# Who makes the low parts of the weight tiles: VectorE alone instead of VectorE and GpSimd, and where they stand around the norms

## The chip, the cores and the metric

The kernel runs on one core of a Trainium2 chip. The time is the device time of one execution in microseconds (us). Engines: TensorE (PE, with PEld for its weight loads), VectorE (DVE), ScalarE (ACT), GpSimd (POOL), and SyncE (SP), whose queue issues most loads.

## What is computed

Four transformer layers over 256 tokens of width 1024, all in float32, batch 1. Layers 0 and 1 are of one model, layers 2 and 3 of another:

```python
# layers 0, 1
proj = x @ w_in[l]                       # 3352 columns, split in 12
mix  = concat([hgrn2(...), nsa(...)]) @ w_out[l]
x = layer_norm(ALPHA * x + mix, ln1_g[l], ln1_b[l])
ffn = (silu(x @ w_gate[l]) * (x @ w_up[l])) @ w_down[l]
x = layer_norm(ALPHA * x + ffn, ln2_g[l], ln2_b[l])
# layers 2, 3
h = rmsnorm(x, attn_norm[l]);  x = x + attention(h) @ w_o[l]
h = rmsnorm(x, ffn_norm[l]);   x = x + conv_ffn(h, ...)
# at the end: rmsnorm(x, final_norm)
```

Layer 2 mixes block attention with an attention over keys that an index score picks (the 64 best of each row); layer 3 adds three dilated patterns.

## The kernel before, in words

**Weights.** All big weights come as one stream of 206 tiles of 128 x 2048 float32 (1 MB each), in the order of use, into three raw buffers (`raw`, SLOTS = 3). A product in full float32 is made of three products in a shorter float: each operand is split into a high part (rounded) and a low part (the remainder), and `products` (lines 695 to 700) adds high by high, high by low and low by high. Each tile is split in two halves of 128 x 1024. ScalarE writes the high part (`split_high`, line 529, the copies at L537). The low part is `raw - w_hi`, two instructions per tile (`take_rest`, L551). It is made by VectorE for most tiles and by GpSimd for the 18 tiles in `on_pool` (lines 268 and 270). The split parts have three buffers too (PARTS = 3), so the split of tile i + 3 is issued right behind the use of tile i: `split_behind(eng, key, ...)` splits the tile that is three after `key`. The load of the tile that goes into a raw buffer waits for the low part of the tile in it (`load`, line 630, through `wait_split`).

**Tiles of GpSimd.** Around each of seven norms, the first and the third of the three tiles that follow the tail of the output product; and behind `nq1` in layers 0 and 1, `k0` and `v2` in layer 2, one tile each (POOL_AFTER).

**Around a norm.** The norms stand behind the output product ("out") and behind the down product ("down") of each layer. Tokens are in two row blocks, tt = 0 and tt = 1, of 128 tokens. TensorE adds up block 0, then block 1. VectorE norms block 0 (`norm(n, 0)`, L1433 to L1462: statistics, then two half rows), then TensorE turns the normed block (`x_transposes`, L762), ScalarE writes the high part of the turned block (`xT_out`, L569, a_hi) and VectorE the low part (L574, a_lo: the "turned remainders"). TensorE then multiplies block 0 with the first two of the new weight tiles (`behind_norm_tiles`, line 721, 24 products per tile), turns block 1 and multiplies it with the same two. So the second use starts no sooner than VectorE has normed block 1. The third new tile is used after that. The norm behind the down product of layer 1 is a double one: norms 3 and 4, a layer norm and an rms norm, one after the other.

The order of work on each engine is written out by hand; each engine runs its instructions in that order and waits on semaphores. Around a norm the order was:

- VectorE: norm of block 0; low part of the second tile; turned remainders of block 0; norm of block 1; turned remainders of block 1.
- ScalarE: root; high parts of the first and second tile; a_hi of block 0 (in the double norm the second root); high part of the third tile; root; a_hi of block 1.
- GpSimd: low part of the first tile; low part of the third tile.

**Layer 2, index attention.** While the projections run, VectorE also adds up index scores (`index_sums`, L1686 and L1688), picks the largest keys (`choose`, L1413 and L1414), takes logits (L1374, L1376) and copies turned probabilities for TensorE (L1387).

**GpSimd besides.** Differences of the decay levels (L1791), a gain (L1798), biases in layer 2 (L1819, L1820), the dilated bias for layer 3 (L1829), and the loads of the norms' gains.

Of the kernel before, what the change touches and what calls it, by code (L numbers as in the profile page):

```python
# [19 lines left out]
ALU = mybir.AluOpType  # L20
ACT = mybir.ActivationFunctionType
AX_X = mybir.AxisListType.X
F32 = mybir.dt.float32
# [10 lines left out]
LAYERS = 4  # L34
PIECES = 2 * NT
TILE = 2048
SLOTS = 3
PARTS = 3
# [197 lines left out]
def tail(l, kind):  # L236

    last = 3 if kind == "out" else FT // 2 - 1
    return [(l, f"{kind}{j}") for j in range(last - TAIL + 1, last + 1)]
# [9 lines left out]
    return key[1] in ("w1k", "w1v")  # L249


POOL_AFTER = {0: ["nq1"], 1: ["nq1"], 2: ["k0", "v2"]}


def turned(key):

    return key is not None and key[1:2] in (("xT",), ("oT",))
# [2 lines left out]
def build(nc, a):  # L260
# [4 lines left out]
    split_tiles = [key for key in stream if not unsplit(key)]  # L265
    split_no = {key: i for i, key in enumerate(split_tiles)}

    on_pool = {split_no[tail(l, kind)[i]] + PARTS for l in range(LAYERS) for kind in ("out", "down") for i in (0, 2)}

    on_pool |= {split_no[(l, n)] + PARTS for l in POOL_AFTER for n in POOL_AFTER[l]}  # L270
    turned_no = {key: i for i, key in enumerate(k for k, _ in bank_uses() if turned(k))}
    assert len(slots) == len(full_no) + 4 * LAYERS and len(tile_no) == len(stream)

    with ExitStack() as ctx:
# [3 lines left out]
        def sem(name):  # L278
            return ctx.enter_context(nc.semaphore(name))
# [118 lines left out]
        rows_used = sem("rows_used")  # L398
        w_hi_done = sem("w_hi_done")
        w_lo_done = sem("w_lo_done")  # L400
        w_lo_pool = sem("w_lo_pool")
        a_hi_done = sem("a_hi_done")
        a_lo_done = sem("a_lo_done")
        w_idx_loaded = sem("w_idx_loaded")
# [100 lines left out]
        def half_tile(i):  # L505
            return slice(i * (TILE // 2), (i + 1) * (TILE // 2))
# [32 lines left out]

        def wait_split(eng, i):  # L540

            mine = i in on_pool
            count = sum((j in on_pool) == mine for j in range(i + 1))
            eng.wait_ge(w_lo_pool if mine else w_lo_done, 2 * count)

        def take_rest(eng, i, done):

            t = tile_no[split_tiles[i]]
            for h in range(2):
                eng.wait_ge(w_hi_done, 2 * i + h + 1)  # L550
                eng.tensor_tensor(w_lo[:, i % PARTS, half_tile(h)], raw[:, t % SLOTS, half_tile(h)],  # L551
                                  w_hi[:, i % PARTS, half_tile(h)].bitcast(F32), ALU.subtract).then_inc(done, 1)

        def split_low(dve, i):
            if i not in on_pool:
                take_rest(dve, i, w_lo_done)

        def split_low_pool(pool, i):
            take_rest(pool, i, w_lo_pool)

        def split_behind(eng, key, split):

            i = split_no[key] + PARTS
            if i < len(split_tiles):
                split(eng, i)
# [511 lines left out]
        def _(act):  # L1077
# [25 lines left out]
            def xT_out(n, tt):  # L1103
                for q in range(2):
                    turned_high(act, (n, "xT", tt, q), a_hi[:, 4 * q:4 * q + 4, tt * P:(tt + 1) * P])

            def around_norm(l, kind, norms):

                keys, turn = tail(l, kind), norms[-1]
                act.activation(nstat[:, 0, 18:19], eps_ln[:, 0:1], ACT.Sqrt)  # L1110
                root(norms[0], 0)
                split_behind(act, keys[0], split_high)
                split_behind(act, keys[1], split_high)
                if len(norms) > 1:
                    root(turn, 0)
                elif turn != 8:
                    xT_out(turn, 0)
                split_behind(act, keys[2], split_high)
                if len(norms) > 1:
                    xT_out(turn, 0)  # L1120
                for n in norms:
                    root(n, 1)
                if turn != 8:
                    xT_out(turn, 1)
# [162 lines left out]
            for l in range(LAYERS):  # L1287
                for name in HEAD_TILES[l]:
                    (tile_out if l < 2 else qkv_out)(l, name)
                for step_ in plan(l):  # L1290
                    kind = step_[0]
# [37 lines left out]
        def _(dve):  # L1329
# [140 lines left out]
            def around_norm(l, kind, norms):  # L1470

                keys, turn = tail(l, kind), norms[-1]
                for n in norms:
                    norm(n, 0)
                split_behind(dve, keys[1], split_low)
                if turn != 8:
                    xT_out(turn, 0)
                for n in norms:
                    norm(n, 1)
                if turn != 8:  # L1480
                    xT_out(turn, 1)

            def feed_forward(l):
                for j in range(HEAD):
# [270 lines left out]
        @block.gpsimd  # L1755
        def _(pool):
            step = steps(pool, pool_step)
            pool.memset(s_hg, 0.0).then_inc(zeroed, 1)
            pool.memset(hid_v[:, :, :], 0.0).then_inc(zeroed, 1)
            pool.memset(cp[:, :, :, :], 0.0).then_inc(zeroed, 1)  # L1760
            pool.memset(ones[:, :], 1.0).then_inc(zeroed, 1)
            pool.memset(eps_ln[:, :], 1e-5)
            pool.memset(eps_rms[:, :], 1e-6).then_inc(zeroed, 1)

            def load_gains(g, b):
                pool.dma_start(gains[:, 0, :], g.partition_broadcast(P)).then_inc(gains_in, 16)
                if b is not None:
                    pool.dma_start(gains[:, 1, :], b.partition_broadcast(P)).then_inc(gains_in, 16)

            def next_gains(n, g, b=None):  # L1770
                pool.wait_ge(normed, n * PIECES)
                load_gains(g, b)

            def around_norm(l, kind):

                keys = tail(l, kind)
                split_behind(pool, keys[0], split_low_pool)
                split_behind(pool, keys[2], split_low_pool)

            load_gains(a["ln1_g"][0], a["ln1_b"][0])  # L1780
            for l in range(2):

                pool.wait_ge(cumsum_done, l + 1)
                for v in range(1, NLEV):
                    n = l * (NLEV - 1) + v
                    half = HALVES[v]
                    if v > 2:
                        pool.wait_ge(level_done, n - 2)
                    src = blocks(f_t, half)
                    mid = src[:, :, half - 1:half].to_broadcast([P, D // (2 * half), 2 * half])  # L1790
                    pool.tensor_tensor(blocks(dec[v % 2], half), src, mid, ALU.subtract).then_inc(diff_done, 1)  # L1791
                for name in POOL_AFTER[l]:
                    split_behind(pool, (l, name), split_low_pool)
                for i in range(2):
                    wait_drained(pool, (l, f"hg{i}"))
                for tt in range(NT):
                    g3 = g_hg[:, tt, :].rearrange("p (h v) -> p h v", h=HG_HEADS)
                    ins = pool.tensor_tensor(g3, g3, bc_mid(gnorm[:, l, :], HG_HEADS), ALU.mult)  # L1798
                ins.then_inc(g_scaled, 1)
                around_norm(l, "out")  # L1800
                next_gains(2 * l + 1, a["ln2_g"][l], a["ln2_b"][l])
                if l == 1:

                    pool.dma_start(gain4, a["rms_g"][0].partition_broadcast(P)).then_inc(gain4_in, 16)
                    pool.dma_start(w_idx_in, a["w_idx"]).then_inc(w_idx_loaded, 16)
                    pool.dma_start(score, a["causal"]).then_inc(score_in, 16)
                around_norm(l, "down")
                if l == 0:
                    next_gains(2, a["ln1_g"][1], a["ln1_b"][1])
            next_gains(5, a["rms_g"][1])  # L1810

            for name in POOL_AFTER[2]:
                split_behind(pool, (2, name), split_low_pool)
            pool.wait_ge(unsel_done, 1)
            for h in range(8):
                if h >= 2:
                    pool.wait_ge(logit_done, 2 * HEADS + 8 + h - 1)
                o = bias_s[h % 2]
                pool.tensor_tensor(o[:, 0:S], bias_of(16 + h, 1), unsel[:, 0:S], ALU.add)  # L1819
                pool.tensor_tensor(o[:, S:TRI], bias_of(16 + h, 0), unsel[:, S:TRI],  # L1820
                                   ALU.add).then_inc(bias_sel, 1)
            around_norm(2, "out")
            next_gains(6, a["rms_g"][2])

            pool.wait_ge(logit_done, 3 * HEADS)
            pool.dma_start(neglog, a["neglog"]).then_inc(neglog_in, 16)
            pool.wait_ge(neglog_in, 16)
            for h in range(16):
                ins = pool.tensor_tensor(bias_t[:, 8 + h, :], bias_t[:, 8 + h, :],  # L1829
                                         neglog, ALU.add)  # L1830
            ins.then_inc(bias_log, 1)
            around_norm(2, "down")
            next_gains(7, a["rms_g"][3])
            around_norm(3, "out")
            next_gains(8, a["final_g"])


# [135 lines left out]
```

## Time and profile before

| | us |
|---|---|
| median of 3 runs | 1594.84 (1592.29 to 1597.41) |
| profiled execution, its own time | 1594.35 |
| profiled execution, span | 1592.6 |
| TensorE busy | 1432.3 (90%) |
| VectorE busy | 975.0 (61%) |
| ScalarE busy | 696.5 (44%) |
| GpSimd busy | 173.2 (11%) |
| 16 DMA engines, queue of the weight stream | 39.2% |

All times of rows are from the start of the span in one profiled execution. An instruction's duration includes the time in which it is held up inside the engine; the time in brackets behind a row is the idle time of the engine before it and what ended it. The granted clock of TensorE (PEclk) has the levels 1.0 and 0.5 of full speed; a number between is a mean over the stretch.

### The profile page before, as it was taken

The numbers are of one execution on the slowest core, as the hardware profiler recorded it, in microseconds if no ns is written. First come the engines' busy times: TensorE is split into PE (matmuls) and PEld (weight loads), VectorE is DVE, ScalarE is ACT, GpSimd is POOL, SyncE is SP. The second block draws the span as 40 slices with busy tenths as digits, with TensorE's granted clock in tenths as the row PEclk, the third lists the DMA queues.
The fourth block names the chain that finished last, engine by engine and source line by source line (L and its number), as shares of the span: only waits on it lengthen the run. The fifth ranks groups of instructions, "written<-read, shape, count | busy, mean of one in ns | idle before, by whom it ended". The sixth has DMA issues, their size and how long they took to land.

```text
span 1592.6 us, 24395 instructions
## 1 busy us (share of the span) xinstructions
PE 1432.3 (90%) x9990; PEld 1334.0 (84%) x9990; DVE 975.0 (61%) x1625; ACT 696.5 (44%) x1136; POOL 173.2 (11%) x114
## 2 busy tenths in 40 slices
PE   6879779999996988899997989879999999799997
PEld 6878669999896977799996989679998898689996
DVE  4555555555757554665557467468767554567767
ACT  4453424333363452443342544245545454245543
POOL 0211020000203200300003013070000200200000
PEclk9879789999997988899997999999999999899999
DMA  8452115555451410455553433144554443235551
GB/s 299 143 213 80 37 70 186 185 185 186 159 184 55 159 54 27 133 212 186 186 185 119 159 107 131 56 149 172 184 200 167 169 149 112 83 138 194 186 208 54
DMA packets 37766, 233.21 MB, mean 146 GB/s; under 512 B 4920, under 2 KB 8712, under 8 KB 11032
## 3 DMA queue, kind: packets, MB, share of 16 engines
q1 hardware_dynamic: 35592, 224.18, 39.2%
q0 software_dynamic: 2064, 7.47, 1.4%
q8 instruction: 80, 1.31, 0.3%
q14 instruction: 30, 0.25, 0.0%
HBM read 230.55 MB, written 1.09 MB: 145 GB/s over the span
## 4 chain that ended last, share of the span: by engine, by line
PE 72%; DVE 17%; ACT 6%; issue 3%; DMA 2%; POOL 1%; DVEq 0%; ACTq 0%
PE bank L698 21%; PE bank L699 21%; PE bank L700 21%; DVE w_lo L551 5%; ACT w_hi L537 2%; PE bank L786 1%; DVE arena L1507 1%; DMA raw<-in_stream 1%; PE bank L798 1%; DVE x L1458 1%; DVE a_lo L574 1%; PE bank L860 1%; DVE res L1456 1%; POOL arena L1791 1%; PE bank L821 1%
## 5 line engine op out<-in xcount | busy, mean ns | idle before, releaser
L551 DVE TENSOR_TENSOR w_lo<-raw,w_hi 128x1024 fp32r<-128x1024 f32 x368 | 457.2, 1286 | 236.0 <-ACT w_hi L537 235.8
L698 PE MATMUL bank<-a_hi,w_hi 128*128 128x256 f32 x1856 | 530.9, 286 | 0.0
L699 PE MATMUL bank<-a_lo,w_hi 128*128 128x256 f32 x1856 | 526.7, 284 | 0.0
L700 PE MATMUL bank<-a_hi,w_lo 128*128 128x256 f32 x1856 | 526.3, 284 | 0.0
L537 ACT ACTIVATE w_hi<-raw 128x1024 fp32r<-128x1024 f32 x404 | 403.3, 1049 | 136.2 <-PE bank L700 79.1
L698 PEld LDWEIGHTS bank<-a_hi,w_hi 128*128 128x128 f32 x1856 | 357.8, 193 | 3.9 <-issue 0.9
L699 PEld LDWEIGHTS bank<-a_lo,w_hi 128*128 128x128 f32 x1856 | 357.7, 193 | 1.3
L700 PEld LDWEIGHTS bank<-a_hi,w_lo 128*128 128x128 f32 x1856 | 357.6, 193 | 0.0
L698 PE MATMUL bank<-w_hi,a_hi 128*128 128x256 f32 (+1 forms) x544 | 190.6, 350 | 51.3 <-DVE a_lo L574 38.8
L551 POOL TENSOR_TENSOR w_lo<-raw,w_hi 128x1024 fp32r<-128x1024 f32 x36 | 94.0, 2634 | 919.2 <-ACT w_hi L537 919.2
L699 PE MATMUL bank<-w_lo,a_hi 128*128 128x256 f32 (+1 forms) x544 | 183.5, 337 | 0.0
L700 PE MATMUL bank<-w_hi,a_lo 128*128 128x256 f32 (+1 forms) x544 | 182.7, 336 | 0.0
L698 PEld LDWEIGHTS bank<-w_hi,a_hi 128*128 128x128 f32 x544 | 117.8, 217 | 65.2 <-issue 47.2
L698 PE MATMUL bank<-w_hi,h_hi 128*128 128x512 f32 x352 | 139.8, 397 | 6.9 <-DVE h_lo L1520 4.1
L699 PE MATMUL bank<-w_lo,h_hi 128*128 128x512 f32 x352 | 140.9, 400 | 0.0
L700 PE MATMUL bank<-w_hi,h_lo 128*128 128x512 f32 x352 | 138.8, 394 | 0.0
L700 PEld LDWEIGHTS bank<-w_hi,a_lo 128*128 128x128 f32 x544 | 117.1, 215 | 7.0
L699 PEld LDWEIGHTS bank<-w_lo,a_hi 128*128 128x128 f32 x544 | 117.9, 217 | 5.9
L1507 DVE SCALAR_TENSOR_TENSOR arena<-bank,conv_col,arena 128x254 f32<-128x254 f32 (+1 forms) x176 | 76.7, 477 | 53.2 <-ACT arena L1148 51.5
L1082 ACT ACTIVATE arena<-bank 128x512 f32<-128x512 f32 (+2 forms) x56 | 32.9, 587 | 133.6 <-PE bank L700 133.5
L698 PEld LDWEIGHTS bank<-w_hi,h_hi 128*128 128x128 f32 x352 | 66.6, 189 | 23.3 <-DVE h_lo L1520 4.5
L700 PEld LDWEIGHTS bank<-w_hi,h_lo 128*128 128x128 f32 x352 | 66.4, 189 | 16.0
(230 smaller groups left out, 1487.4 us busy)
## 6 DMA issues: line engine op xcount, KB each, us to landing
raw<-in_stream SPq DMA_DIRECT2D x206, 1024.0 KB, 4.8
bias_t<-bias_rows SPq DMA_DIRECT2D x6, 512.0 KB, 7.5
gains<-in_ln_g POOLq DMA_DIRECT2D x4, 512.0 KB, 4.3
gains<-in_ln_b POOLq DMA_DIRECT2D x4, 512.0 KB, 6.3
gains<-in_rms_g POOLq DMA_DIRECT2D x3, 512.0 KB, 4.0
res<-in_xT SPq DMA_DIRECT2D x1, 1024.0 KB, 4.9
x<-in_x SPq DMA_DIRECT2D x1, 1024.0 KB, 8.3
out<-res SPq DMA_DIRECT2D x2, 512.0 KB, 2.6
```

What stands on the lines that cost most here:

```text
L537: act.activation(w_hi[:, i % PARTS, half_tile(h)], raw[:, t % SLOTS, half_tile(h)], ACT.Copy).then_inc(w_hi_done, 1)
L551: eng.tensor_tensor(w_lo[:, i % PARTS, half_tile(h)], raw[:, t % SLOTS, half_tile(h)], w_hi[:, i % PARTS, half_tile(h)].bitcast(F32), ALU. ...
L574: dve.tensor_tensor(part, bank_of(key).rearrange("p (i t) -> p i t", i=part.shape[1]), high.bitcast(F32), ALU.subtract).then_inc(*drained( ...
L698: pe.matmul(out, lh, rh, start=first, stop=False)
L699: pe.matmul(out, lh, rl, start=False, stop=False)
L700: return pe.matmul(out, ll, rh, start=False, stop=last)
L786: mm = pe.matmul(out[:, c:c + P], lhs[:, c:c + P], rhs[:, c:c + P], start=True, stop=True)
L798: mm = pe.matmul(b[:, 32 * i:32 * i + 30], w[:, k, :], blk[i][:, k, :, :].rearrange("p g n -> p (g n)"), start=(k == 0), stop=(k == CMP_KT ...
L821: mm = pe.matmul(b[:, c:c + NC], nq[lo:lo + DH, j, tt * P:(tt + 1) * P], kc2[lo:lo + DH, j // 2, :], start=True, stop=True)
L860: pe.matmul(b[i][:, 0:S], q[i][:, P:S], k[i], start=True, stop=True)
L1082: act.activation(dst, bank_of(key) if src is None else src, ACT.Copy, scale=scale).then_inc(*drained(key))
L1507: ins = dve.scalar_tensor_tensor(c[:, lag:], b[:, i * S:(i + 1) * S - lag], conv_col[:, m, i * FT + j, tap:tap + 1], c[:, lag:], ALU.mult, ...
```

## The change

GpSimd makes no low parts any more; VectorE makes those of all tiles, in the order of the stream, and one semaphore counts them. Behind `nq1`, `k0` and `v2` VectorE makes them at the place where it skipped them. Around a norm the order is new:

- VectorE: norm of block 0; low part of the first tile; turned remainders of block 0; low part of the second tile; norm of block 1; turned remainders of block 1; low part of the third tile.
- ScalarE: root; high part of the first tile; (second root in the double norm); a_hi of block 0; high parts of the second and third tile; root; a_hi of block 1.

```diff
-POOL_AFTER = {0: ["nq1"], 1: ["nq1"], 2: ["k0", "v2"]}
...
-    on_pool = {split_no[tail(l, kind)[i]] + PARTS for l in range(LAYERS) for kind in ("out", "down") for i in (0, 2)}
-    on_pool |= {split_no[(l, n)] + PARTS for l in POOL_AFTER for n in POOL_AFTER[l]}
...
         def wait_split(eng, i):
-            mine = i in on_pool
-            count = sum((j in on_pool) == mine for j in range(i + 1))
-            eng.wait_ge(w_lo_pool if mine else w_lo_done, 2 * count)
+            eng.wait_ge(w_lo_done, 2 * (i + 1))
...
+        def split_low(dve, i):
             t = tile_no[split_tiles[i]]
             for h in range(2):
-                eng.wait_ge(w_hi_done, 2 * i + h + 1)
-                eng.tensor_tensor(w_lo[:, i % PARTS, half_tile(h)], raw[:, t % SLOTS, half_tile(h)],
-                                  w_hi[:, i % PARTS, half_tile(h)].bitcast(F32), ALU.subtract).then_inc(done, 1)
+                dve.wait_ge(w_hi_done, 2 * i + h + 1)
+                dve.tensor_tensor(w_lo[:, i % PARTS, half_tile(h)], raw[:, t % SLOTS, half_tile(h)],
+                                  w_hi[:, i % PARTS, half_tile(h)].bitcast(F32), ALU.subtract).then_inc(w_lo_done, 1)
...
# ScalarE, around_norm
                 split_behind(act, keys[0], split_high)
-                split_behind(act, keys[1], split_high)
                 if len(norms) > 1:
                     root(turn, 0)
-                elif turn != 8:
+                if turn != 8:
                     xT_out(turn, 0)
+                split_behind(act, keys[1], split_high)
                 split_behind(act, keys[2], split_high)
-                if len(norms) > 1:
-                    xT_out(turn, 0)
...
# VectorE, around_norm
                 for n in norms:
                     norm(n, 0)
-                split_behind(dve, keys[1], split_low)
+                split_behind(dve, keys[0], split_low)
                 if turn != 8:
                     xT_out(turn, 0)
+                split_behind(dve, keys[1], split_low)
                 for n in norms:
                     norm(n, 1)
                 if turn != 8:
                     xT_out(turn, 1)
+                split_behind(dve, keys[2], split_low)
...
# GpSimd
-            def around_norm(l, kind):
-                keys = tail(l, kind)
-                split_behind(pool, keys[0], split_low_pool)
-                split_behind(pool, keys[2], split_low_pool)
...
-                for name in POOL_AFTER[l]:
-                    split_behind(pool, (l, name), split_low_pool)
...
-                around_norm(l, "out")
...
-                around_norm(l, "down")
```

## Rows read from the trace of the kernel before

**Rows 1.** Page: engines busy, chain of waits, GpSimd's subtractions, a load (KB, us).
```profile
PE 1432.3 (90%) x9990; PEld 1334.0 (84%) x9990; DVE 975.0 (61%) x1625; ACT 696.5 (44%) x1136; POOL 173.2 (11%) x114
...
PE 72%; DVE 17%; ACT 6%; issue 3%; DMA 2%; POOL 1%; DVEq 0%; ACTq 0%
...
L551 POOL TENSOR_TENSOR w_lo<-raw,w_hi 128x1024 fp32r<-128x1024 f32 x36 | 94.0, 2634 | 919.2 <-ACT w_hi L537 919.2
...
raw<-in_stream SPq DMA_DIRECT2D x206, 1024.0 KB, 4.8
```

**Rows 2.** Timeline (start, duration, instruction), VectorE, norm behind layer 0's output product.
```profile
225.88 2.96 DVE L1458 SCALAR_TENSOR_TENSOR x<-res,nstat,gains 128x512 f32<-128x512 f32 x1
228.77 2.84 DVE L1456 SCALAR_TENSOR_TENSOR res<-res,nstat,gains 128x512 f32<-128x512 f32 x1
...
232.31 2.35 DVE L551 TENSOR_TENSOR w_lo<-raw,w_hi 128x1024 fp32r<-128x1024 f32 x2
234.58 1.28 DVE L574 TENSOR_TENSOR a_lo<-bank,a_hi 128x512 fp32r<-128x512 f32 x2
235.78 0.67 DVE L1433 SCALAR_TENSOR_TENSOR res<-x,bank 128x512 f32<-128x512 f32 x1
...
241.68 0.75 DVE L1458 SCALAR_TENSOR_TENSOR x<-res,nstat,gains 128x512 f32<-128x512 f32 x1
```

**Rows 3.** Timeline, GpSimd and TensorE, same norm.
```profile
225.89 5.17 POOL L551 TENSOR_TENSOR w_lo<-raw,w_hi 128x1024 fp32r<-128x1024 f32 x2 [60.36 <-ACT w_hi L537]
...
235.41 0.55 PE L698 MATMUL bank<-w_hi,a_hi 128*128 128x256 f32 x1 [2.13 <-DVE a_lo L574]
...
245.26 0.36 PE L698 MATMUL bank<-w_hi,a_hi 128*128 128x256 f32 x1 [1.07 <-DVE a_lo L574]
```

**Rows 4.** Timeline, norm behind layer 0's down product, VectorE and TensorE.
```profile
427.51 4.55 DVE L551 TENSOR_TENSOR w_lo<-raw,w_hi 128x1024 fp32r<-128x1024 f32 x2
...
439.20 0.75 DVE L1458 SCALAR_TENSOR_TENSOR x<-res,nstat,gains 128x512 f32<-128x512 f32 x1
...
440.78 0.36 PE L698 MATMUL bank<-w_hi,a_hi 128*128 128x256 f32 x1
```

**Rows 5.** Timeline, double norm behind layer 1's down product.
```profile
844.74 2.78 DVE L1458 SCALAR_TENSOR_TENSOR x<-res,nstat,gains 128x512 f32<-128x512 f32 x1
...
851.65 6.65 DVE L551 TENSOR_TENSOR w_lo<-raw,w_hi 128x1024 fp32r<-128x1024 f32 x2
...
871.22 0.55 PE L698 MATMUL bank<-w_hi,a_hi 128*128 128x256 f32 x1 [0.84 <-DVE a_lo L574]
```

**Rows 6.** Timeline, norm behind layer 2's output product.
```profile
1038.21 5.40 DVE L551 TENSOR_TENSOR w_lo<-raw,w_hi 128x1024 fp32r<-128x1024 f32 x2 [1.23 <-ACT w_hi L537]
...
1048.76 1.42 DVE L1462 SCALAR_TENSOR_TENSOR res<-x,nstat,gains 128x512 f32<-128x512 f32 x2
...
1054.20 0.36 PE L698 MATMUL bank<-w_hi,a_hi 128*128 128x256 f32 x1 [1.07 <-DVE a_lo L574]
```

**Rows 7.** Windows: us; busy of PE, PEld, DVE, ACT, POOL; clock; DMA; GB/s.
```profile
245.20:251.20 6.00, 5.94 (x50) 5.97 (x50) 1.74 (x3) 2.49 (x3) 0.00 (x0) 1.00 0.35 115
859.00:867.40 8.40, 8.34 (x48) 8.16 (x48) 7.77 (x14) 0.30 (x1) 0.00 (x0) 0.68 0.66 252
```

**Rows 8.** Timeline, layer 0, VectorE behind nq1.
```profile
129.89 1.31 DVE L1353 COPY_PREDICATED arena<-hg_mask,bank 128x1024 f32<-128x1024 uint8 x1 [4.57 <-PE bank L786]
```

**Rows 9.** Timeline, layer 2: VectorE and TensorE behind k0, TensorE behind v2.
```profile
922.50 1.42 DVE L1686 SCALAR_TENSOR_TENSOR arena<-arena,gates 128x256 f32<-128x256 f32 x1 [3.58 <-ACT arena L1277]
923.83 2.46 DVE L1688 SCALAR_TENSOR_TENSOR arena<-arena,gates 128x128 f32<-128x128 f32 x1
926.39 0.48 DVE L1686 SCALAR_TENSOR_TENSOR arena<-arena,gates 128x256 f32<-128x256 f32 x1
...
930.59 0.70 PE L893 MATMUL bank<-arena 64*128 64x256 f32 x4 [2.39 <-ACT arena L1277]
...
964.05 0.41 PE L882 MATMUL bank<-arena,pT 128*128 128x64 f32 x2 [1.13 <-DVE pT L1387]
```

More of the change, by code:

```diff
@@ L400, in build @@
         w_lo_done = sem("w_lo_done")
-        w_lo_pool = sem("w_lo_pool")
         a_hi_done = sem("a_hi_done")
@@ L540, in wait_split @@
         def wait_split(eng, i):
-            mine = i in on_pool
-            count = sum((j in on_pool) == mine for j in range(i + 1))
-            eng.wait_ge(w_lo_pool if mine else w_lo_done, 2 * count)
-        def take_rest(eng, i, done):
+            eng.wait_ge(w_lo_done, 2 * (i + 1))
+        def split_low(dve, i):
             t = tile_no[split_tiles[i]]
             for h in range(2):
-                eng.wait_ge(w_hi_done, 2 * i + h + 1)
-                eng.tensor_tensor(w_lo[:, i % PARTS, half_tile(h)], raw[:, t % SLOTS, half_tile(h)],
-                                  w_hi[:, i % PARTS, half_tile(h)].bitcast(F32), ALU.subtract).then_inc(done, 1)
[L554 to L559, printed above, removed]
+                dve.wait_ge(w_hi_done, 2 * i + h + 1)
+                dve.tensor_tensor(w_lo[:, i % PARTS, half_tile(h)], raw[:, t % SLOTS, half_tile(h)],
+                                  w_hi[:, i % PARTS, half_tile(h)].bitcast(F32), ALU.subtract).then_inc(w_lo_done, 1)
         def split_behind(eng, key, split):
@@ L1810, in _ @@
             next_gains(5, a["rms_g"][1])
-            for name in POOL_AFTER[2]:
-                split_behind(pool, (2, name), split_low_pool)
             pool.wait_ge(unsel_done, 1)
@@ L1821, in _ @@
                                    ALU.add).then_inc(bias_sel, 1)
-            around_norm(2, "out")
             next_gains(6, a["rms_g"][2])
@@ L1831, in _ @@
             ins.then_inc(bias_log, 1)
-            around_norm(2, "down")
             next_gains(7, a["rms_g"][3])
-            around_norm(3, "out")
             next_gains(8, a["final_g"])
```

## The prediction, as it was put on record before the run

> **What bounds the kernel now.** I read the page first: TensorE is busy 90% of the span, and the chain of waits that ended last is TensorE for 72% and VectorE for 17%, with GpSimd at 1% [rows 1]. So the kernel is a stream of products with places where TensorE stands and VectorE is the one it stands for. GpSimd's 36 subtractions (18 tiles, two halves each) take 94.0 us on GpSimd, 2.63 us each [rows 1]. Taken by engine shares they look free. I then asked for the waits of TensorE by stretch, and for the timeline of all engines around each of the seven norms at which GpSimd subtracts, and at the other four tiles.
>
> The timeline shows that they aren't free. In the first norm VectorE's scaling of a half row takes 0.75 us when GpSimd is quiet (at 241.68) but 2.96 and 2.84 us at 225.88 and 228.77; these start just as GpSimd's pair of subtractions does and end with its two halves [rows 2, 3]. That is 2.2 + 2.1 = 4.3 us of VectorE standing still inside instructions, on the path norm, turned block, a_lo, first product. The same shows at the tile's own subtractions: two halves take 2.35 us on VectorE alone [rows 2], 4.55 [rows 4], 6.65 [rows 5] and 5.40 us [rows 6] with GpSimd on its own pair. Instructions that read PSUM for one input aren't held: L1433 took 0.67 us at 235.78 and a_lo 1.28 for two, while GpSimd made its second tile [rows 2].
>
> **What of it counts.** The products of block 1 (tt = 1) start when VectorE has normed block 1. In the norm behind layer 0's down product the last scaling ends at 439.20 + 0.75 = 439.95 and the first product of block 1 starts at 440.78 [rows 4]: 0.83 us later. I call this the norm-bound start. Where TensorE came to block 1 later than that, it was still at the products of block 0, and there is slack: in layer 0's first norm 245.26 - (241.68 + 0.75 + 0.83) = 2.0 us [rows 2, 3], and in layer 2's first 1054.20 - (1048.76 + 1.42 + 0.83) = 3.2 us [rows 6].
>
> **The seven norms.** In the new order VectorE does, ahead of the norm of block 1, one pair of halves more (2.35 us), and loses the stalls.
> - Layer 0, out: stalls 4.3, less 2.35: norm of block 1 starts about 1.9 us sooner. The products of block 0 start at about 231.1 in place of 235.41 (norm of block 0 done at 225.88 + 3 x 0.75 = 228.1, first tile's low part at 230.4, the first a_lo 0.65 later) and no longer cover block 1, so the 2.0 of slack come too: 3.9 us. The high part of the second tile, now behind a_hi on ScalarE, is wanted 24 products after 231.1, at 234 or later, and VectorE has its low part by 234.1. Layer 1, out, is of the same form: 3.9.
> - Layer 0, down: 2.0 in one L1458 (as the 2.78 - 0.75 of [rows 5]) and 2.2 in the subtractions (4.55 - 2.35 [rows 4]), less 2.35: 1.9, and no slack; with a small hold in the second norm 2.0 us.
> - Layer 1, down (double norm): 2.03 in L1458 and 4.3 in the subtractions [rows 5], less 2.35: 4.0, and some 0.4 in a small instruction between; 4.4 us off the start at 871.22.
> - Layer 2, out: 5.40 - 2.35 = 3.05 in the subtractions, and VectorE's idle 1.23 us before them [rows 6] is now used; less 2.35 and less some 0.7 for waits on a_hi and on the second tile's high part, which ScalarE makes later: 1.2. Plus the slack 3.2 (0.2 kept back for the first half row): 4.2 us. Layer 3, out, has the same form: 4.2.
> - Layer 2, down: between the down norm of layer 0 and the out norm of layer 2, as TensorE has the last rows to add between the turns and the products: 3.1.
> Sum: 3.9 + 3.9 + 2.0 + 4.4 + 4.2 + 4.2 + 3.1 = 25.7 us.
>
> **TensorE's clock.** 48 products took 5.94 us at clock 1.00, and 8.34 us at a mean of 0.68, behind a stand of 5.89 us [rows 7]: 2.4 us more. After 1.07 us of idle they ran at 1.00 (the start at 245.26 [rows 3, 7]). Before, the slow ones were mostly those of block 0. In the new order block 0 starts sooner and is done sooner, and then TensorE waits 2 to 4 us for the norm of block 1, so in some norms the slow level (1.2 GHz) will fall on the products of block 1, which count. Bounds: 0 and 7 x 2.4 = 17 us. I take 4 us, nearer to 0, because the wait is broken by the turns of the first half, and because where block 0 itself runs slow it fills the wait.
>
> **The third tile.** Its low part moves behind the turned remainders of block 1. TensorE wants it 48 products (5.94 us [rows 7]) after that start, and VectorE has it 1.28 + 2.35 us after the norm, some 3 us early: nothing. Its raw buffer comes free about 5 us later than from GpSimd, so SyncE issues the load of the tile three further that much later, with everything behind it in its queue; a load lands 4.8 us after issue [rows 1], and the tile's high part is written only behind the use of the third tile, more than 10 us on: nothing.
>
> **The other four tiles.** Behind nq1 in layers 0 and 1 VectorE stood idle 4.57 us for TensorE [rows 8], and the pair fits there: 0. Behind k0 in layer 2 GpSimd held an index sum for 1.42 + 2.46 us where the next pair starts with 0.48 and goes on at a like rate, about 3.1 us of stall; VectorE's own pair costs about 1.1 net of its idle time before: 2.0 us gained, of the 2.39 that TensorE stood [rows 9]. Behind v2 VectorE works without a gap at choosing keys, with nothing in it that GpSimd held, so 2.35 us go straight into the wait for pT (1.13 before [rows 9]), which becomes 3.5; with such a stand the clock may fall, 1.3 more. Net of layer 2: +1.7 us; bounds -2.0 (the pair at v2 absorbed) and +4 (k0 brings nothing, v2 all).
>
> **A page on this.** The Trainium skill, SBUF — State Buffer, section Who interferes with whom, has GpSimd and a VectorE instruction with two SBUF inputs share one read interface, held for the whole instruction, so that the other blocks fully. Taken by that, each of the some 16 held instructions would lose a whole GpSimd half (5.17 / 2 = 2.6 us), not 2.1 to 2.2, and with some 6 us more in the sum the time would be 1568, on the side of the second rival. The rows measure the stall itself, so I keep to them.
>
> **Sum.** -25.7 + 4.0 + 1.7 = -20.0 us. The profiled execution took 1594.35 us (0.49 less than the median of the runs shown): 1574.4 us. All of the gain lies on the path in places where TensorE stood, and what follows (feed-forward products at clock 1.00) is shifted as a whole.
>
> **Rivals.**
> - The clock eats most of it: the slow level falls on block 1 in nearly all norms (some 12 us) and layer 2 costs 4: -25.7 + 12 + 3 = -11: 1584. For it: TensorE's wait before block 1 gets longer in all seven. Against it: the start at 440.78 followed a norm-bound wait and was at full clock. Chance 0.15.
> - More than that: no clock loss, and layer 2 even: 1594.4 - 27.7 = 1567. Chance 0.17.
> - The stalls aren't GpSimd's doing, but come with the loads that land then; GpSimd's leaving changes nothing for them, while the new order still swaps places: within 0.3%. Against it: the holds start and end with GpSimd's halves. Chance 0.03.
> - Slower: the third tile. If its raw buffer, free some 5 us later, is what the stream waits for, then every norm loses 5 us at the tile three further and the gain at the norm is given back and more: 7 x 5 = 35 us against 20 gained: 1609. It decides when the load lands later than ScalarE's turn at it; of the 10 us above 4.8 go to the load, so some 5 us of room are left, and the DMA engines' share is at 0.35 to 0.66 [rows 7]. Chance 0.05.
> - The forecast: 0.60.
>
> About 0.3% (5 us) is what a measurement of this kernel can tell from no change. Range: from 1564 (the third case with its bounds) to 1584. Faster 0.92, within 0.3% 0.03, slower 0.05.
>
> **What would show it.** GpSimd has no L551 and some 80 us busy. VectorE's L551 has 404 instructions at a mean of about 1.2 us. L1456, L1458 take 0.75 us in all norms. The first product of block 0 follows the norm some 4 us sooner in each out norm, and 7 in the double one; the first product of block 1 starts about 0.8 us behind the last scaling in all seven. The wait of L882 for pT in layer 2 grows to 3 us or more. Wrong would be: a scaling longer than 1 us with no GpSimd near it, a wait of L698 for the third tile, or a slow clock in block 1 everywhere.

## The result: 1574.07 us, and the profile after

The changed kernel takes 1574.07 us (median of 4 runs, 1571.35 to 1574.62), the kernel before in the same comparison 1594.41 us: a ratio of 0.9867, 95% interval 0.9848 to 0.9887. It is 20.3 us faster; 1574.4 was forecast. The profiled execution has a span of 1572.8 us.

The page of the changed kernel, which answers to [rows 1]: busy times, the chain of waits, VectorE's low parts, a load.
```profile
PE 1428.0 (91%) x9990; PEld 1329.7 (85%) x9990; DVE 985.0 (63%) x1661; ACT 696.8 (44%) x1136; POOL 77.6 (5%) x78
...
PE 72%; DVE 17%; ACT 5%; issue 3%; DMA 2%; POOL 1%; DVEq 0%; SPq 0%; ACTq 0%
...
L542 DVE TENSOR_TENSOR w_lo<-raw,w_hi 128x1024 fp32r<-128x1024 f32 x404 | 484.3, 1243 | 225.7 <-ACT w_hi L530 225.0
...
raw<-in_stream SPq DMA_DIRECT2D x206, 1024.0 KB, 4.9
```
GpSimd's subtractions are gone. VectorE got 36 of them, some 42 us of work by the 2.35 us that a pair takes, and is busy only 10 us longer: for the other 32 us it had stood still inside its own instructions. The chain has nearly the shares of before, so it does not tell where 20 us went; the timelines do.

VectorE in the norm behind layer 0's output product, changed kernel (start, duration, instruction), which answers to [rows 2]:
```profile
222.91 0.75 DVE L1438 SCALAR_TENSOR_TENSOR res<-res,nstat,gains 128x512 f32<-128x512 f32 x1
223.70 0.76 DVE L1440 SCALAR_TENSOR_TENSOR x<-res,nstat,gains 128x512 f32<-128x512 f32 x1
...
225.82 2.35 DVE L542 TENSOR_TENSOR w_lo<-raw,w_hi 128x1024 fp32r<-128x1024 f32 x2
228.09 1.28 DVE L558 TENSOR_TENSOR a_lo<-bank,a_hi 128x512 fp32r<-128x512 f32 x2
229.28 2.35 DVE L542 TENSOR_TENSOR w_lo<-raw,w_hi 128x1024 fp32r<-128x1024 f32 x2
231.55 0.68 DVE L1415 SCALAR_TENSOR_TENSOR res<-x,bank 128x512 f32<-128x512 f32 x1
...
237.32 0.75 DVE L1440 SCALAR_TENSOR_TENSOR x<-res,nstat,gains 128x512 f32<-128x512 f32 x1
...
240.58 2.35 DVE L542 TENSOR_TENSOR w_lo<-raw,w_hi 128x1024 fp32r<-128x1024 f32 x2
```
TensorE there, and in the norms behind layer 0's down product, layer 1's down product (double) and layer 2's output product, one after the other; these answer to [rows 3 to 6]. In brackets is the idle time before a row:
```profile
228.92 0.36 PE L682 MATMUL bank<-w_hi,a_hi 128*128 128x256 f32 x1 [1.92 <-DVE a_lo L558]
...
236.77 0.63 PE L746 MATMUL bank<-ident,x 128*128 128x128 f32 x4 [1.86 <-DVE x L1440]
...
238.96 0.56 PE L682 MATMUL bank<-w_hi,a_hi 128*128 128x256 f32 x1
...
432.51 0.63 PE L746 MATMUL bank<-ident,x 128*128 128x128 f32 x4 [1.08 <-DVE x L1440]
...
434.64 0.36 PE L682 MATMUL bank<-w_hi,a_hi 128*128 128x256 f32 x1
...
846.70 0.36 PE L682 MATMUL bank<-w_hi,a_hi 128*128 128x256 f32 x1 [2.24 <-DVE a_lo L558]
...
859.00 1.94 PE L746 MATMUL bank<-ident,res 128*128 128x128 f32 x8 [6.33 <-DVE res L1444]
861.60 0.55 PE L682 MATMUL bank<-w_hi,a_hi 128*128 128x256 f32 x1 [0.65 <-DVE a_lo L558]
...
1041.64 1.29 PE L746 MATMUL bank<-ident,res 128*128 128x128 f32 x8 [1.39 <-DVE res L1444]
1043.77 0.36 PE L682 MATMUL bank<-w_hi,a_hi 128*128 128x256 f32 x1 [0.84 <-DVE a_lo L558]
```
The 2.96 and 2.84 us of [rows 2] are 0.75 us now, and each pair of subtractions takes 2.35. TensorE is done with block 0 before VectorE has normed block 1, so it stands ahead of the turns (L746): 1.9, 1.1, 6.3 and 1.4 us.

I took the n-th product of TensorE in both traces and the difference of their starts (after less before). Its steps over the places of the prediction, in us:

| place | predicted | measured |
|---|---|---|
| layer 0: out, down | -3.9, -2.0 | -2.6, -2.2 |
| layer 1: out, down | -3.9, -4.4 | -1.8, -3.9 |
| layer 2: out, down | -4.2, -3.1 | -3.9, -3.9 |
| layer 3: out | -4.2 | -4.6 |
| clock behind the norms | +4 | (within the rows above) |
| layer 2 at k0; at v2 | -2.0; +3.7 | -2.1; +3.9 |
| elsewhere | 0 | +1.4 |
| sum | -20.0 | -19.7 |

"Elsewhere" is -1.3 up to layer 0's norm, +2.4 inside layer 1, +1.0 in layer 2 beside the two tiles and -0.75 in its feed-forward part. TensorE ran the same instructions there, and slow stretches of its clock fell at other moments. In layer 1 one wait for VectorE grew as well, from 1.31 to 2.92 us: TensorE came to it sooner, out of faster products, and VectorE's work ahead of it was bound by ScalarE.

TensorE's clock in block 1's products, changed kernel (us; busy of PE, PEld, DVE, ACT, POOL; clock; DMA share; GB/s), in the norms of layer 0 out and down, layer 1 out and down, and layer 2 out (the third row starts with the turns of the second half row):
```profile
238.90:244.90 6.00, 6.00 (x32) 6.00 (x32) 2.96 (x3) 1.05 (x2) 0.59 (x2) 0.55 0.62 199
434.64:440.64 6.00, 6.00 (x50) 6.00 (x51) 4.23 (x5) 3.07 (x4) 0.52 (x1) 1.00 0.71 220
657.52:663.52 6.00, 6.00 (x39) 6.00 (x40) 3.49 (x4) 1.64 (x3) 2.70 (x5) 0.74 0.75 184
861.60:869.31 7.71, 7.71 (x50) 7.71 (x51) 4.22 (x5) 2.49 (x3) 0.00 (x0) 0.75 0.55 192
1043.77:1049.77 6.00, 6.00 (x50) 6.00 (x51) 4.07 (x4) 2.49 (x3) 3.06 (x4) 1.00 0.63 214
```
50 products in 6.00 us at 2.4 GHz, 32 in the same time where most of it was at 1.2. Before, layer 0's block 1 ran at 1.00 [rows 7]: this is why that norm gave 2.6 us of 3.9. (At the start of block 1 it was 5.0 us ahead, 0.8 of them from a slow stretch that no longer fell just ahead of the norm; the slow products took 2.4 back.) In the double norm block 1 ran at the lower level for a while in the kernel before, too:
```profile
871.20:878.60 7.40, 7.38 (x49) 7.40 (x50) 1.70 (x3) 2.49 (x3) 0.00 (x0) 0.77 0.20 68
```
So against the kernel before, block 1's 48 products take longer by 2.4 us in layer 0's out norm, 1.1 in layer 1's and 0.2 in the double one: 3.7 us, and nothing in the other four.

Layer 2 behind v2, where VectorE's new pair has no cover; TensorE's row and the clock behind it, answering to the last of [rows 9]:
```profile
954.33 0.66 PE L866 MATMUL bank<-arena,pT 128*128 128x64 f32 x2 [3.42 <-DVE pT L1369]
```
```profile
954.30:959.30 5.00, 4.97 (x23) 5.00 (x24) 4.73 (x15) 2.46 (x5) 0.00 (x0) 0.50 0.01 2
```

### The profile page after: what moved, and what is told of

Read it like the earlier page. It is cut to its first block, busy times and chain, and to the rows that moved or that the text cites. A ratio compares the mean times of both kernels' runs of the same rounds, so it can differ in the third digit from the quotient of the medians.

```text
span 1572.8 us, 24395 instructions
## 1 busy us (share of the span) xinstructions
PE 1428.0 (91%) x9990; PEld 1329.7 (85%) x9990; DVE 985.0 (63%) x1661; ACT 696.8 (44%) x1136; POOL 77.6 (5%) x78
## 3 DMA queue, kind: packets, MB, share of 16 engines
q8 instruction: 80, 1.31, 0.3%
## 4 chain that ended last, share of the span: by engine, by line
PE 72%; DVE 17%; ACT 5%; issue 3%; DMA 2%; POOL 1%; DVEq 0%; SPq 0%; ACTq 0%
PE bank L682 21%; PE bank L683 21%; PE bank L684 21%; DVE w_lo L542 5%; DMA raw<-in_stream 2%; ACT w_hi L530 2%; PE bank L770 2%; DVE arena L1491 1%; PE bank L782 1%; PE bank L844 1%; DVE a_lo L558 1%; DVE nstat L1420 1%; DVE x L1440 1%; PE bank L868 1%; PE bank L867 1%
## 5 line engine op out<-in xcount | busy, mean ns | idle before, releaser
L542 DVE TENSOR_TENSOR w_lo<-raw,w_hi 128x1024 fp32r<-128x1024 f32 x404 | 484.3, 1243 | 225.7 <-ACT w_hi L530 225.0
L682 PE MATMUL bank<-w_hi,a_hi 128*128 128x256 f32 (+1 forms) x544 | 186.3, 343 | 32.1 <-DVE a_lo L558 19.7
L683 PE MATMUL bank<-w_lo,a_hi 128*128 128x256 f32 (+1 forms) x544 | 179.6, 330 | 0.0
L684 PE MATMUL bank<-w_hi,a_lo 128*128 128x256 f32 (+1 forms) x544 | 178.3, 328 | 0.0
L682 PEld LDWEIGHTS bank<-w_hi,a_hi 128*128 128x128 f32 x544 | 113.3, 208 | 45.1 <-issue 27.2
L684 PEld LDWEIGHTS bank<-w_hi,a_lo 128*128 128x128 f32 x544 | 112.9, 208 | 7.1
L683 PEld LDWEIGHTS bank<-w_lo,a_hi 128*128 128x128 f32 x544 | 113.3, 208 | 5.7
L1212 ACT ACTIVATE lbuf<-lbuf,mxn 128x256 f32<-128x256 f32 x64 | 32.6, 509 | 106.5 <-DVEq L1360 106.0
```

Of the source, the lines that this page charges most:

```text
L542: dve.tensor_tensor(w_lo[:, i % PARTS, half_tile(h)], raw[:, t % SLOTS, half_tile(h)], w_hi[:, i % PARTS, half_tile(h)].bitcast(F32), ALU. ...
L682: pe.matmul(out, lh, rh, start=first, stop=False)
L683: pe.matmul(out, lh, rl, start=False, stop=False)
L684: return pe.matmul(out, ll, rh, start=False, stop=last)
L1212: act.activation(e[:, 0:S], e[:, 0:S], ACT.Exp, scale=-1.0, bias=mxn[:, half, 1, h:h + 1], accum_out=esum[:, half, 1, h:h + 1])
```

## The experiments

Twelve kernels ran, in three comparisons, in which the kernel before took 1594.05, 1592.63 and 1594.45 us; differences of 1 or 2 us between kernels of different comparisons mean nothing. The theory: GpSimd's subtractions hold those VectorE instructions that read two inputs in SBUF, and taking them away frees VectorE's path to the norm of block 1. The rivals: the order is what gains; the stalls aren't GpSimd's; the clock takes the gain.

**The move and the order, each alone.** "engine_alone" is the changed kernel with the old order:
```diff
 split_behind(dve, keys[0], split_low)
+split_behind(dve, keys[1], split_low)
 if turn != 8:
     xT_out(turn, 0)
-split_behind(dve, keys[1], split_low)
```
(and ScalarE's order of before). 

> All low parts on VectorE, but around the norms the order of before: both low parts of the first two tiles stand ahead of the turned remainders of block 0 (and ScalarE has the old order too). If the gain is GpSimd's holds going away, nearly all of it stays: VectorE reaches the norm of block 1 at the same time as in the changed kernel, block 0's products start 2.35 us later, and that only shows where TensorE waited less than 2.35 us ahead of block 1 (1.86, 1.86, 1.08, 6.33, 1.39, 1.40 and 0 us in the seven norms): at most 0.5+0.5+1.3+0+1.0+1.0+2.35 = 6.6 us, of which TensorE's clock gives some back as it stands for less: 1578 us, range 1574 to 1581. If the new order is what gains, this kernel stays near the one before: 1590 us or more.

Measured: 1578.76 us, ratio 0.9899 (0.9886 to 0.9912). As expected: the move alone gives 1.0% of the 1.3%. By its trace each out norm of layers 2 and 3 gives some 1.5 us less than with the new order, those of layers 0 and 1 no less. There TensorE starts block 0 some 2.3 us later and no longer waits ahead of block 1; in layer 0 block 1 then starts 1.4 us later than in the changed kernel, but runs at full clock, which gives more back ("engine_alone", columns as above):
```profile
240.89:246.89 6.00, 6.00 (x50) 6.00 (x51) 3.99 (x5) 2.49 (x3) 0.00 (x0) 1.00 0.74 259
```

"order_alone" is the kernel before with the new order on VectorE and ScalarE, GpSimd's tiles left where they were. 

> The kernel before with the new order alone: turned remainders of block 0 ahead of the second tile's low part on VectorE and of its high part on ScalarE; GpSimd keeps its 18 tiles. If the holds are the cause, they stay, and VectorE has the same instructions ahead of block 1's norm as before, so its start doesn't move; block 0 starts 2.4 to 5.4 us sooner, which gives only the slack ahead of block 1: 2.0 us in each of the first two out norms, 3.2 in the last two, nothing in the down norms: at most 10.4 us, 1587 us, range 1584 to 1592. If the order is what gains: 1575 us.

Measured: 1596.78 us, ratio 1.0012 (1.0003 to 1.0021). The side was right (no gain from order alone), my number was 10 us off: not 7 us faster, but 2 slower. VectorE in the norm of layer 0's output, "order_alone":
```profile
225.01 2.96 DVE L1456 SCALAR_TENSOR_TENSOR x<-res,nstat,gains 128x512 f32<-128x512 f32 x1
...
233.26 0.69 DVE L574 TENSOR_TENSOR a_lo<-bank,a_hi 128x512 fp32r<-128x512 f32 x1 [1.14 <-ACT a_hi L569]
234.20 2.36 DVE L551 TENSOR_TENSOR w_lo<-raw,w_hi 128x1024 fp32r<-128x1024 f32 x2 [0.25 <-ACT w_hi L537]
...
240.01 1.69 DVE L1454 SCALAR_TENSOR_TENSOR res<-res,nstat,gains 128x512 f32<-128x512 f32 x1
```
The turned remainder comes before its high part is there, so VectorE idles for 1.14 and 0.25 us, and GpSimd's second pair slides beside the scaling of block 1 (1.69 for 0.75 us). From the held scaling to the end of the norm VectorE takes 2.4 us more than in the kernel before. Block 1's products also run slower: 48 take 7.45 us for 5.82. In the changed kernel the first low part fills the time that VectorE idles here: the order pays only once that work is VectorE's. The parts of the change don't add up: -1.0% and +0.1% alone, -1.3% together.

**The four tiles outside the norms.** "four_tiles_alone" is the kernel before with `POOL_AFTER = {0: [], 1: [], 2: []}`. 

> The kernel before, of whose GpSimd tiles only the four outside the norms (behind nq1 in layers 0 and 1, behind k0 and v2 in layer 2) go to VectorE. By the two traces k0 gives 2.1 us and v2 costs 3.9, nq1 nothing: 1596.2 us, range 1594 to 1598.5. If those two readings are only the phase of TensorE's clock, the time is that of before, 1594.4 us, or anything within 3 us of it.

Measured: 1595.36 us, ratio 1.0006 (0.9997 to 1.0015): by the median alone undecided. Its trace has both steps: -2.1 us at k0, +3.8 at v2.

"v2_on_gpsimd" is the changed kernel with v2's low part back on GpSimd (`POOL_AFTER = {2: ["v2"]}`, no tile around the norms). 

> The changed kernel, with one tile's low part (the one behind v2 in layer 2, among the choosing of keys) back on GpSimd. If VectorE's pair there goes straight into the wait for pT and lets the clock fall, 2.35 to 3.9 us come back: 1570.5 us, range 1569 to 1572.5. If GpSimd's pair holds the choosing of keys as long as VectorE's own pair takes, nothing changes: 1574 us.

Measured: 1568.13 us, ratio 0.9828 (0.9813 to 0.9842), 5.9 us below the changed kernel and 1 below the range expected; the two intervals don't overlap. VectorE beside GpSimd's pair (945.30 to 950.04 us), then TensorE behind v2 and the clock there:
```profile
945.10 0.43 DVE L1411 MAX8 stat<-arena 128x8 f32<-128x256 f32 x1
...
945.64 0.41 DVE L1412 MATCH_REPLACE8 arena<-stat,arena 128x256 f32<-128x256 f32 x1
...
953.52 0.41 PE L882 MATMUL bank<-arena,pT 128*128 128x64 f32 x2 [1.15 <-DVE pT L1385]
```
```profile
953.50:958.50 5.00, 4.98 (x43) 5.00 (x44) 4.73 (x15) 2.46 (x4) 0.00 (x0) 1.00 0.12 49
```
Choosing reads one input in SBUF and isn't held; the wait is 1.15 us again for 3.42, and the clock stays at 1.00 where the changed kernel has 0.50. The 3.9 us of this place are shown; some 2 us more came from the clock elsewhere.

"v2_v3_on_gpsimd" adds v3's tile. 

> The version with v2's tile on GpSimd, and v3's beside it: VectorE's pair at 956.62 us stands among the choosing of keys, and TensorE waits 1.24 us for pT at 962.73. The choosing (one input in SBUF) was not held by GpSimd's pair at 945.3 us. If that holds here too, the 1.24 us go, and no more, since the wait is shorter than the pair: 1567 us. If GpSimd is late with the low part for TensorE, or its index sums start late behind it: 1568 us or above.

Measured: 1566.63 us, ratio 0.9832 (0.9811 to 0.9854). The wait for pT behind v3 is gone from its trace, but against the version with v2 alone nothing can be told.

**What holds VectorE.** Three kernels add idle work on GpSimd to the changed kernel, at the four moments of each norm at which it subtracted before; nobody waits for it. For two inputs:
```diff
+pool.wait_ge(w_hi_done, 2 * i + h + 1)
+spoil(pool.tensor_tensor(part, part, ones[:, 0:1].unsqueeze(2).to_broadcast([P, 4, S]), ALU.mult))
```
for one input `pool.tensor_copy(part, part)`, for writing alone 16 times `pool.memset(spare[:, :], 0.0)`. `part` is 128x1024 elements.

> The changed kernel; added is idle work on GpSimd: at each norm, as soon as the high parts of the first and of the third tile are written (where GpSimd subtracted in the kernel before), four products of 128x1024 elements of a constant table with ones, two inputs in SBUF, result back in the same place. None of its results is waited for. If GpSimd's reading holds VectorE, the scalings go back to 2.8 to 2.96 us and the low parts beside it grow by 2.2 us: the holds of before were worth 20.6 us gained + 7 x 2.35 of added work = 37 us, so 1611 us, range 1600 to 1625. If the holds came from something else in the subtractions (the tiles' own buffers, the loads that land then), the time stays at 1574 us.

> As the one with two inputs, but GpSimd's idle work is a copy of 128x1024 elements (one input in SBUF) at the same four places of each norm. If it is the second input that VectorE and GpSimd compete for, 1574 us and scalings of 0.75 us; if any reading by GpSimd holds VectorE, some 1611 us as with two inputs, less if the copy is shorter.

> As the one with two inputs, but GpSimd's idle work only writes: 16 fills of 128x160 elements at each of the four places of each norm, no input at all. If reading is what holds VectorE: 1574 us, scalings of 0.75 us. If any use of SBUF by GpSimd holds it: over 1590 us.

Measured: 1610.71 us (ratio 1.0110, 1.0094 to 1.0126), 1589.46 (0.9972, 0.9959 to 0.9984) and 1584.31 (0.9948, 0.9931 to 0.9964). Norm behind layer 0's output: one of VectorE's held scalings and GpSimd's pair, two inputs, then one input, then the fills:
```profile
225.28 2.39 DVE L1439 SCALAR_TENSOR_TENSOR res<-res,nstat,gains 128x512 f32<-128x512 f32 x1
...
224.68 4.74 POOL L1770 TENSOR_TENSOR bias_t<-bias_t,ones 128x1024 f32<-128x1024 f32 x2 [58.82 <-ACT w_hi L531]
```
```profile
225.73 1.52 DVE L1439 SCALAR_TENSOR_TENSOR res<-res,nstat,gains 128x512 f32<-128x512 f32 x1
...
225.14 3.02 POOL L1770 COPY bias_t<-bias_t 128x1024 f32<-128x1024 f32 x2 [58.81 <-ACT w_hi L531]
```
```profile
225.81 0.75 DVE L1440 SCALAR_TENSOR_TENSOR res<-res,nstat,gains 128x512 f32<-128x512 f32 x1
...
225.19 18.48 POOL L1772 MEMSET spare<- 128x160 f32 x64 [58.79 <-ACT w_hi L532]
```
With two inputs the time lands on the 1611 us expected, though the work touches none of the weights' buffers: the stalls are GpSimd's reading. By the steps of the traces some 32 us of the loss stand in the seven norms; 3 more come behind layer 1's out norm, where TensorE waits 1.83 us for a low part. One input on GpSimd is enough. VectorE's instruction ends 0.6 us behind GpSimd's half in both (227.67 against 224.68 + 2.37; 227.25 against 225.14 + 1.51): it waits for the end of GpSimd's instruction and then does its own work. So what is lost is what is left of GpSimd's instruction, less 0.1 to 0.2 us: 1.77 left and 1.64 lost, 0.92 left and 0.77 lost.

Two inputs on VectorE aren't the condition for it. In the changed kernel GpSimd's biases in layer 2 run until 1062.23 (GpSimd, then the same VectorE instruction beside and behind them):
```profile
1046.70 15.53 POOL L1800 TENSOR_TENSOR bias_t<-bias_t,arena 128x256 f32<-128x256 f32 x16 [3.16 <-DMA arena<-in_neglog]
```
```profile
1060.05 0.72 DVE L1503 TENSOR_SCALAR h_hi<-arena 128x256 fp32r<-128x256 f32 x1
...
1064.28 0.29 DVE L1503 TENSOR_SCALAR h_hi<-arena 128x256 fp32r<-128x256 f32 x1
```
Of the kernel's 88 instructions of this kind it is the only one beside which GpSimd works on such inputs, and the other 87 take 0.29 to 0.30 us. In "gpsimd_writes", where the biases run until 1071.13, the second of the two takes 0.70 us as well.

The fills hold nothing, and still cost some 10 us (13 by the ratios): neither of the two answers expected. Their 18.5 us put GpSimd's loads of gains and of layer 2's tables behind them. Behind layer 1's out norm VectorE waits for one of these tables (w_idx) ahead of its next low parts, and TensorE for those. VectorE in the changed kernel, then VectorE and TensorE in "gpsimd_writes":
```profile
668.28 0.50 DVE L1512 TENSOR_SCALAR w_idx_hi<-arena 128x640 fp32r<-128x640 f32 x1 [6.05 <-DMA arena<-in_w_idx]
```
```profile
670.51 0.49 DVE L1514 TENSOR_SCALAR w_idx_hi<-arena 128x640 fp32r<-128x640 f32 x1 [10.20 <-DMA arena<-in_w_idx]
...
674.28 0.55 PE L684 MATMUL bank<-a_hi,w_hi 128*128 128x256 f32 x1 [4.24 <-DVE w_lo L544]
```
This wait of 4.24 us isn't in the changed kernel. With a slow stretch behind it the step there is 6.3 us, and another 2.1 stand in layer 2's feed-forward part, where GpSimd's biases start 11 us later (5 of them the shift up to there), so that two VectorE instructions ahead of a product are held, and the wait for it is 3.69 us for 2.95, with a slow stretch behind. I took the late loads for the cause and halved the fills. 

> As the fills on GpSimd before, but half as many: 8 fills of 128x160 at each of the four places of a norm. The 16 took 18.5 us per norm and put GpSimd's loads of the gains and of layer 2's tables 17 us later, into the stream of weights, where one tile came late by some 6 us; no instruction of VectorE was longer. With half of them the loads leave in time. If writing by GpSimd holds nothing: 1574 us, range 1572 to 1577. If the loss of 10 us was the writing itself, half of it stays: 1579 us.

Measured: 1574.76 us (ratio 0.9877, 0.9847 to 0.9908), the changed kernel's time. The interval is wide (1570 to 1580 us) and takes in the other answer, 1579; the traces decide. No scaling is longer than 0.75 us in either, and with half the fills the wait of 4.24 us is down to 0.29. So writing holds nothing; what cost was GpSimd's other work coming late. The expectation had their size wrong: the first of them left 2.3 us later than in the changed kernel (659.93 for 657.67), not 17, and it was the table that came late, not a tile of the weights.

**The clock.** Two kernels give TensorE idle products where it stands ahead of block 1's turns, into a bank that is free then:
```diff
+for i in range(FILL.get(n, 0)):
+    pe.matmul(bank[:, 4, 0:S], a_hi[:, i % KT, 0:P], w[:, i % KT, :], start=True, stop=True)
 x_transposes(n, 1)
```


> The version with v2's tile on GpSimd (1568.1 us), and TensorE makes idle products (128x256, into a bank that is free then) where it stood before the turns of block 1: 15, 8, 15, 50, 11, 0 and 11 of them in the seven norms, about as long as it stood there. If the standing is what lets TensorE's clock fall on block 1's products, these go back to 5.9 us for 48: 2.4 us at layer 0's out norm, some 3 at layer 1's, 2.3 at the double one, nothing at the others: 1560.5 us, range 1556 to 1565. If the idle products don't lift the clock, or only move the slow stretch: 1568 us. If they overrun and delay the turns: above 1568 us.

Measured: 1565.98 us, ratio 0.9827 (0.9813 to 0.9842): the ratio of the same kernel without them, 0.9828, and not the 1560.5 us expected if the gains of the norms stay. Its trace takes 1.0 and 2.0 us off layer 1's norms and gives them back where the clock now falls: 3.0 us between 1010 and 1020 us, 2.4 at 1356. In layer 0's norm the slow stretch came on block 0, the idle products ran over, and block 1 started 1.1 us later than in the changed kernel.

> The changed kernel with idle products of TensorE (128x256) where it stood before the turns of block 1: 15, 8, 15, 50, 11, 0 and 11 in the seven norms. With v2's tile on GpSimd the same products took some 3 us out of the norms and the median stayed, since slow stretches came up elsewhere. If the clock that a wait costs is only moved, this kernel too stays within 3 us of the changed kernel: 1574 us, range 1571 to 1576. If each slow stretch behind a wait is a loss of its own, 8 us come off: 1566 us.

Measured: 1568.57 us, ratio 0.9832 (0.9817 to 0.9846), between the two answers: 5.5 us below the changed kernel. Block 1's products in the norms of layer 0 out, layer 1 out and layer 1 down, "after_filled":
```profile
239.80:245.80 6.00, 6.00 (x50) 6.00 (x51) 4.26 (x5) 3.05 (x4) 0.57 (x2) 1.00 0.63 231
656.30:662.30 6.00, 6.00 (x50) 6.00 (x51) 2.96 (x3) 3.05 (x4) 2.15 (x5) 1.00 0.87 234
858.77:864.77 6.00, 6.00 (x50) 6.00 (x51) 4.06 (x5) 2.49 (x3) 0.00 (x0) 1.00 0.57 190
```
All three are at 1.00 now, and these norms give 2.4, 1.1 and 2.2 us, 5.7 in all; the norms that were at full clock before give nothing. So slow products of block 1 did cost the changed kernel some 6 us (of which 2 in the double norm, most of them there before the change, too), and the fill can get it back. But the two traces also differ by 3 us in places without fills, and the kernel with v2's tile on GpSimd kept nothing: whether a given kernel keeps it depends on where its slow stretches fall.

**The third tile's place.** "third_tile_early" is the changed kernel with its low part ahead of the norm of block 1. 

> The changed kernel with the third tile's low part ahead of the norm of block 1 on VectorE. If block 1's start is bound by that norm in all seven places, each loses VectorE's 2.35 us, 16.5 us in all, less some us where it waits for ScalarE or the clock gives back: 1589 us, range 1583 to 1593. If TensorE has slack there (block 0's products as cover) the loss is under half of that: below 1582 us.

Measured: 1600.51 us, ratio 1.0036 (1.0022 to 1.0050): 26.4 us, not 15. TensorE ahead of block 1's turns and the products behind, layer 0 down, "third_tile_early":
```profile
438.91 1.09 PE L746 MATMUL bank<-ident,x 128*128 128x128 f32 x4 [3.35 <-DVE x L1440]
```
```profile
441.50:449.00 7.50, 7.50 (x50) 7.50 (x51) 1.96 (x3) 3.08 (x4) 0.06 (x1) 0.77 0.46 142
```
The wait is 3.35 us for 1.08, and 50 products take 7.50 us at 0.77 where the changed kernel has 6.00 at 1.00. By the steps of the traces the norms lose 2.4 and 4.2 us in layer 0, 1.8 and 3.0 in layer 1, 5.3 and 4.7 in layer 2 and 5.3 in layer 3. All are bound by the norm: the expectation of 2.35 us each held for the work itself, in the three where the clock was down already. In the other four the longer wait dropped it too, and the price doubled.

## Why the prediction was right, point by point

- **GpSimd holds VectorE**: shown by the rows, and by "gpsimd_two_inputs", which brings the stalls back with other data. The Trainium skill, SBUF — State Buffer, section Who interferes with whom, says that a VectorE instruction with two inputs in SBUF contends with a GpSimd instruction that reads there, not with one that only writes, and that one with a single input, outside VectorE's 2-port modes, doesn't contend: the copy (1.52 us), the fills (0.75) and MAX8 (0.43) agree. L1503 (0.72 us for 0.29), with one input and held all the same, doesn't fit unless it ran in such a mode, which no run here shows. The full block of that section agrees, too; my estimate from it, 2.6 us an instruction and 1568 us, was the mistake, as it took GpSimd's half whole, not what was left of it.
- **The norms**: 22.9 us measured against 21.7 (25.7 less 4 for the clock). Three came out clearly lower, layer 0 out, layer 1 out and layer 1 down, each with block 1 at a clock of 0.55 to 0.75, and layer 2 out by 0.3; the down norms of layers 0 and 2 and layer 3 came out higher, by 0.2, 0.8 and 0.4 us.
- **The clock, 4 us**: 3.7 us against the kernel before, on top of which come steps of 1 to 2.4 us in places that the change doesn't touch. The term was a choice between 0 and 17, so its closeness is in part luck; that those steps nearly cancelled (+1.4) is luck outright. The rival that the clock eats most of the gain didn't come.
- **The norm-bound start, 0.83 us behind the last scaling**: 0.89 and 0.83 us in layer 0 (238.96 - 238.07, 434.64 - 433.81), but 1.6 in layer 2 (1043.77 - 1042.16) and 2.1 in the double norm (861.60 - 859.52). "In all seven" was wrong, and 0.83 us is no constant: the start hangs on the first half row. From its turns (L746) to the first product it is 2.19 and 2.13 us in layer 0, 2.13 in layer 2, and 2.60 in the double norm, at the lower clock. The last scaling ends 1.3 us behind the start of these turns in layer 0, but 0.5 in layer 2, whose two scalings follow each other without others between them. So the slack of 3.2 us in layer 2's out norm was 2.4 (1054.20 - 1050.18 - 1.61). The sum hid it: VectorE reached the end of that norm 1.7 us sooner, net of the shift, and not 1.2. That the forecast of 4.2 us met 3.9 there is two errors that cancel.
- **First product of block 0**: net of the shift up to there 5.2 us sooner in layer 0 (said: 4; 0.8 of them are the slow stretch ahead of the norm), 6.9 in the double norm (7), 3.7 in layer 2 (4).
- **The third tile, nothing**: right; no product waits for it, and "third_tile_early" shows what its place is worth.
- **nq1, nothing**: TensorE's wait behind it is 1.38 us in both layers, for 1.41 and 1.40 before.
- **k0 and v2**: -2.1 and +3.9 for -2.0 and +3.65. At k0 the wait of 2.39 us is 0.29 now, at v2 that of 1.13 is 3.42. Each step is shown by a kernel that moves or keeps it, with 3.8 us at v2 where it is moved alone and none where it is kept.
- **The rival that the stalls aren't GpSimd's, only the order matters**: closed from both sides, by "engine_alone" and "order_alone".

## What to carry to other kernels

Cost a small engine's work by what it does to its neighbour's instructions, not by its own share: 94 us on an engine that was busy for 11% held VectorE for some 37 us on the path (an estimate: 20 us gained, and 7 x 2.35 us of new work paid; GpSimd's idle reading in "gpsimd_two_inputs" costs as much). Give GpSimd work beside VectorE instructions that it didn't hold here: those that chose keys and those with one of their two inputs from PSUM. Reading one input in SBUF isn't enough (L1503: 0.72 us for 0.29), so look up each instruction in a trace. GpSimd's writes held nothing. v2's tile among the choosing of keys is a good place: left there, the kernel takes 1568.1 us. An order can cost 2 us alone and be worth 5 beside a new placement: try them together before dropping either.

## What was unexpected of the hardware

- GpSimd's copy, with one input, holds VectorE as its subtraction does: 1.52 us for a scaling of 0.75 us.
- A wait of TensorE can cost twice when it gets long: behind waits of 1.1 and 1.4 us ahead of block 1's turns the products ran at 1.00, behind 1.9 and 6.3 us at 0.55 to 0.75, behind the 3.35 us of "third_tile_early" at 0.77. There 2.35 us of added work cost 4.2 us and more. The length of the wait doesn't settle it: in "gpsimd_one_input" block 1 ran at 1.00 behind 1.94 us (layer 0 down), in "gpsimd_writes" at 0.77 behind 1.40 (layer 2 out).
- Idle products in place of a wait bring block 1 to full clock (0.55, 0.74, 0.75 to 1.00), yet of two kernels that differ in one tile one kept the 5.5 us and one kept nothing. Steps of 1 to 3 us came and went in stretches with the same instructions.
